# Halved first weight blocks in the projections, two norms made one stage earlier, semaphores cleared by range

## The reference

```python
h = rms_norm(x, mix_norm_g)
u = h @ w_in                                   # 1024 x 4096
dq, dk, dv, bq, bk, bv, z = split(u)
dq, dk, bq, bk = rms_norm of each over 64-wide heads
a = diff_attention(dq, dk, dv, lam, slopes)    # 4 heads; bias -slope * |distance|; softmax 1 - lam * softmax 2
b = dilated_attention(bq, bk, bv, slopes)      # 8 heads, windows 128/512/2048 at dilation 1/4/16
x = x + (concat(rms_norm(a) * 0.8, b) * silu(z)) @ w_out
x = x + sigmoid(rms_norm(x, ple_norm_g) @ w_ple_gate) * (p @ w_ple_proj)
# second block: sliding window attention with sinks
xn = rms_norm(x, norm_g_2)
q, k, v, z = split(xn @ a_w_in_2)
x = x + (banded_attention(q, k, v, t5_table, 128, sinks) * silu(z)) @ a_w_out_2
return rms_norm(x, final_g_2)
```

## Time and profile before

| what | value |
|---|---|
| median of 3 runs | 3131.64 us (3131.01 to 3131.96) |
| profiled execution | 3134.61 us, span 3132.8 us |
| TensorE products busy | 2984.1 us, 95% of the span |
| VectorE busy | 1656.2 us, 53% |
| ScalarE busy | 1195.8 us, 38% |
| GpSimd busy | 729.7 us, 23% |
| DMA | 302.94 MB, mean 97 GB/s |
| stages' ends (all engines meet) | p 786.0, d 1385.0, l 1754.0, m 1983.2, g 2235.7, s 2712.7, w 3128.9 |

### The profile page before, as it was taken

How to read it: one execution, slowest core, us unless ns; L and a number is a source line. 1 busy time by engine, 2 the same in 40 slices (tenths; PEclk the granted TensorE clock), 3 DMA queues, 4 the chain that set the end, 5 groups by cost and what they waited for, 6 DMA issues and landing times. The chain is left out here.

```text
span 3132.8 us, 47888 instructions
## 1 busy us (share of the span) xinstructions
PE 2984.1 (95%) x18330; PEld 2489.8 (79%) x18330; DVE 1656.2 (53%) x2757; ACT 1195.8 (38%) x2667; POOL 729.7 (23%) x576
## 2 busy tenths in 40 slices
PE   6999999999799999989999799899799999799998
PEld 6988888988588888878888678688688888667776
DVE  3366665000888888866666677433341100166665
ACT  3222221011577777755555321322211111255553
POOL 1234433110502010027452344200001110121111
PEclk9999999999899999999999899999899999899999
DMA  4212212223212010022332556332245542544341
GB/s 155 84 58 71 72 60 78 72 64 74 82 28 50 22 48 22 22 77 86 100 101 68 200 211 240 128 123 82 82 124 118 126 96 52 159 150 140 127 152 64
DMA packets 254270, 302.94 MB, mean 97 GB/s; under 512 B 19376, under 2 KB 201696, under 8 KB 250848
## 3 DMA queue, kind: packets, MB, share of 16 engines
q1 hardware_dynamic: 254048, 299.92, 31.7%
HBM read 190.38 MB, written 109.47 MB: 96 GB/s over the span
## 5 line engine op out<-in xcount | busy, mean ns | idle before, releaser
L890 DVE CUSTOM_DVE_ANT_0 d_e<-d_score,d_dist,d_slope 128x1024 f32<-128x1024 f32 x256 | 318.5, 1281 | 62.9 <-PE d_score L953 62.9
L561 PE MATMUL p_acc<-p_h_hi,p_w_hi 128*128 128x512 f32 x768 | 300.0, 391 | 1.0 <-issue 1.0
L561 PE MATMUL p_acc<-p_h_hi,p_w_lo 128*128 128x512 f32 x768 | 299.5, 390 | 0.0
L561 PE MATMUL p_acc<-p_h_lo,p_w_hi 128*128 128x512 f32 x768 | 299.1, 389 | 0.0
L812 ACT ACTIVATE d_e<-d_e,d_neg_top 128x2048 f32<-128x2048 f32 x128 | 257.0, 2008 | 86.5 <-DVE d_neg_top L899 86.2
L504 DVE RECIPROCAL p_root<-p_root 128x512 f32<-128x512 f32 x64 | 214.6, 3353 | 123.0 <-ACT p_root L417 123.0
L976 PE MATMUL d_out<-d_v,d_w_t 128*128 128x128 f32 x2048 | 251.5, 277 | 0.0
L976 PEld LDWEIGHTS d_out<-d_v,d_w_t 128*128 128x128 f32 x2048 | 240.9, 194 | 0.0
L561 PE MATMUL s_acc<-s_h_hi,s_w_hi 128*128 128x512 f32 x576 | 224.7, 390 | 0.0
L561 PE MATMUL s_acc<-s_h_hi,s_w_lo 128*128 128x512 f32 x576 | 224.4, 390 | 0.0
L561 PE MATMUL s_acc<-s_h_lo,s_w_hi 128*128 128x512 f32 x576 | 224.4, 390 | 0.0
(11 more groups left out here) (277 smaller groups left out, 6907.4 us busy)
## 6 DMA issues: line engine op xcount, KB each, us to landing
k_carry<-in_w_in SPq DMA_DIRECT2D x16, 1024.0 KB, 6.0
cols<-k_carry SPq DMA_DIRECT2D x64, 256.0 KB, 2.4
w_q<-q SPq DMA_DIRECT2D x15, 1024.0 KB, 7.8
k_carry<-x SPq DMA_DIRECT2D x27, 512.0 KB, 3.6
o_parts<-l_stage SPq DMA_DIRECT2D x192, 66.0 KB, 1.7
m_o<-o_parts SPq DMA_DIRECT2D x48, 264.0 KB, 6.0
k_carry<-cols SPq DMA_DIRECT2D x48, 256.0 KB, 4.6
k_carry<-in_a_w_in SPq DMA_DIRECT2D x10, 1024.0 KB, 5.6
```

The costliest lines, as they stand in the source:

```text
L561: mm = pe.matmul(acc[:, room], w_part[:, j, kt, ct * P:(ct + 1) * P], h_part[:, kt, tc * BANK:(tc + 1) * BANK], start=(kt == 0 and m == 0) ...
L890: dve.tensor_tensor_reduce(e[:, m % 3, s, half * HALF:(half + 1) * HALF], score[:, 2 * half:2 * half + 2].rearrange("p a b -> p (a b)"), d ...
```

## The change

Eight edits: (1) `Phase.clear` clears each run of neighbouring semaphore numbers with one instruction. (2) The first two weight blocks of a projection are loaded, rounded and subtracted in halves of four rows of 128; VectorE makes all four low halves, GpSimd none. (3) TensorE begins unit 0 with tile 0 and the first half of block 0; the transposes of tile 1 stand between the fourth and fifth step. A unit of the "rows" kind waits for each of its two tiles by itself. (4) `norm(t + 2)` no longer stands between the low parts of two tiles but behind both. (5) The eight gain loads move behind unit 7. (6) In the second projection the factors of tiles 2 to 15 are a power on GpSimd instead of root and reciprocal, and tiles 0 and 1 are normed in the gate stage, behind its tile 14. (7) The first k of diff attention is split in halves. (8) The fold of the distances goes to ScalarE as an absolute value; the signs of slope and of the diff gains are turned for it.

```diff
     def clear(self):
-        for counter in self.counters:
-            self.nc.gpsimd.sem_clear(counter)
+        nums = sorted(counter.num for counter in self.counters)
+        first = nums[0]
+        for num, following in zip(nums, nums[1:] + [None]):
+            if following != num + 1:
+                self.nc.gpsimd.sem_clear(range(first, num + 1))
+                first = following
...
     def load_w(self, sp, i):
-        sp.dma_start(self.w_raw[:, i % 2], self.w_b[self.blocks[i][0]]).then_inc(self.w_loaded[i % 2], 16)
+        src = self.w_b[self.blocks[i][0]]
+        if i < 2:
+            for half in range(2):
+                at = slice(4 * half, 4 * half + 4)
+                sp.dma_start(self.w_raw[:, i, at], src[:, at]).then_inc(self.w_first_loaded[2 * i + half], 16)
+        else:
+            sp.dma_start(self.w_raw[:, i % 2], src).then_inc(self.w_loaded[i % 2], 16)
...
# GpSimd, projection
-                invert_mean(0)
-                invert_mean(1)
-            make_lo(1)
+                for t in range(4):
+                    invert_mean(t)
+            else:
+                rest = inv[:, 2:NT]
+                pool.tensor_scalar(rest, sq_sums[:, 2:NT], 1.0 / D, EPS, ALU.mult, ALU.add).then_inc(rooted, 1)
+                pool.wait_ge(rooted, 1)
+                pool.tensor_tensor(rest, rest, half_down[:, 0:1].to_broadcast([P, NT - 2]), ALU.pow).then_inc(inverted, 1)
...
# ScalarE, projection
             if sq_sums is None:
                 square(0)
+            make_first_hi(0, 0)
+            make_first_hi(0, 1)
+            keep_hi(0)
+            if sq_sums is None:
                 square(1)
-            else:
-                act.activation(inv[:, 0], sq_sums[:, :], ACT.Sqrt, bias=eps[:, 0:1], scale=1.0 / D).then_inc(rooted, 1)
-            make_hi(0)
-            keep_hi(0)
-            make_hi(1)
+            make_first_hi(1, 0)
+            keep_hi(1)
+            make_first_hi(1, 1)
+            if sq_sums is None:
+                square(2)
+                square(3)
...
# VectorE, projection
-            norm(0)
-            norm(1)
-            dve.wait_ge(w_hi_made, 1)
-            dve.tensor_tensor(w_lo[:, 0], w_raw[:, 0], w_hi[:, 0].bitcast(F32), ALU.subtract).then_inc(w_lo_made, 1)
+            if sq_sums is None:
+                norm(0)
+            make_first_lo(0, 0)
+            keep_lo(0)
+            make_first_lo(0, 1)
+            if sq_sums is None:
+                norm(1)
+                make_first_lo(1, 0)
+                keep_lo(1)
+                make_first_lo(1, 1)
+                norm(2)
+                norm(3)
+            else:
+                norm(2)
+                keep_lo(1)
+                norm(3)
+                make_first_lo(1, 0)
+                make_first_lo(1, 1)
...
# TensorE, projection
                 for t in tiles_before(n):
-                    transposes(t)
-                pe.wait_ge(lo_kept, needs[n] + 1)
-                if n == first_of[i]:
-                    pe.wait_ge(w_lo_made, i + 1)
+                    if t != 1:
+                        transposes(t)
...
                     for two in range(2):
+                        pe.wait_ge(lo_kept, 2 * k + two + 1)
                         for kt in range(KT):
+                            if two == 0:
+                                wait_weights(n, i, kt)
+                            if n == 0 and two == 0 and kt == 4:
+                                transposes(1)
...
# diff attention, ScalarE (VectorE's fold and its whole-k subtraction go)
+            def fold(n, first, last):
+                act.wait_ge(counted, n + 1)
+                counts = e[:, 2].rearrange("p b n -> p (b n)")[:, first:last]
+                act.activation(dist[:, first:last], counts, ACT.Abs).then_inc(dist_made, 1)
+
             act.wait_ge(k_loaded, 64)
-            act.activation(k_hi[:, 0], k_raw[:, :], ACT.Copy).then_inc(k_hi_made, 1)
+            for s in range(2):
+                act.activation(k_hi[:, 0, s], k_raw[:, s], ACT.Copy).then_inc(k_first_hi, 1)
+            fold(0, NEAR, SPAN)
+            fold(1, 0, NEAR)
...
# gate stage, GpSimd
+            pool.wait_ge(squared, 2)
+            pool.tensor_scalar(first, sq_sums3[:, 0:2], 1.0 / D, EPS, ALU.mult, ALU.add).then_inc(next_set, 1)
+            pool.wait_ge(next_set, 2)
+            pool.tensor_tensor(first, first, swa_inputs.half_down[:, 0:1].to_broadcast([P, 2]), ALU.pow)\
+                .then_inc(next_rooted, 1)
...
# gate stage, VectorE
+                if isinstance(t, int) and t == NT - 2:
+                    dve.wait_ge(next_rooted, 1)
+                    dve.wait_ge(swa_inputs.gain_loaded, 16)
+                    for n in range(2):
+                        dve.wait_ge(swa_inputs.x_loaded[n], 16)
+                        dve.scalar_tensor_tensor(
+                            out=swa_inputs.x_slots[n], in0=swa_inputs.x_slots[n], scalar=swa_inputs.inv[:, n:n + 1],
+                            in1=swa_inputs.gain_all[:, :].rearrange("p (a b n) -> p a b n", a=2, n=P),
+                            op0=ALU.mult, op1=ALU.mult).then_inc(swa_inputs.first_normed, 1)
```

More of the change, by code:

```diff
@@ L317, in _ @@
                 inputs.load_x(sp, 2)
[L318 to L322, removed]
             for n, (i, k) in enumerate(units):
@@ L328, in _ @@
                 if n == first_of[i] and i + 2 < len(blocks):
-                    sp.wait_ge(w_lo_made, i + 1)
+                    sp.wait_ge(w_lo_made, 2 * (i + 1))
                     inputs.load_w(sp, i + 2)
+                if qk is not None and n == 8:
+                    for item, g in enumerate(qk):
+                        for half in range(2):
+                            sp.dma_start(g_raw[half * HD:(half + 1) * HD, item:item + 1], column(g),
+                                         allow_slow_non_contiguous=True).then_inc(qk_loaded, 16)
                 sp.wait_ge(staged[n % ROOMS], n // ROOMS + 1)
@@ L380, in _ @@
                     for t in tiles_before(n):
-                        if t + 2 < NT:
+                        if 2 <= t and t + 2 < NT:
                             invert_mean(t + 2)
@@ L470, in keep_lo, with make_first_lo @@
                                   h_hi[:, :, at].bitcast(F32), ALU.subtract).then_inc(lo_kept, 1)
-                if t + 2 < NT:
-                    norm(t + 2)
+            def make_first_lo(i, half):
+                at = slice(4 * half, 4 * half + 4)
+                dve.wait_ge(w_hi_made, 2 * i + half + 1)
+                dve.tensor_tensor(w_lo[:, i, at], w_raw[:, i, at], w_hi[:, i, at].bitcast(F32), ALU.subtract)\
+                   .then_inc(w_lo_made, 1)
             def fill_gains():
@@ L496, in _ @@
                 for t in tiles_before(n):
-                    keep_lo(t)
+                    if t >= 2:
+                        keep_lo(t)
+                for t in tiles_before(n):
+                    if 2 <= t and t + 2 < NT:
+                        norm(t + 2)
                 if kind == "head_norm":
@@ L524, in transposes @@
             def transposes(t):
-                pe.wait_ge(normed, t + 1)
+                if sq_sums is None:
+                    pe.wait_ge(normed, t + 1)
+                elif t < 2:
+                    pe.wait_ge(first_normed, t + 1)
+                else:
+                    pe.wait_ge(normed, t - 1)
                 if t >= 2:
@@ L851, in _ @@
         def _(dve):
-            def fold(n, first, last):
-                dve.wait_ge(counted, n + 1)
-                counts = e[:, 2].rearrange("p b n -> p (b n)")[:, first:last]
-                dve.scalar_tensor_tensor(out=dist[:, first:last], in0=counts, scalar=-1.0, in1=counts, op0=ALU.mult,
-                                         op1=ALU.min).then_inc(dist_made, 1)
             def lambda_sums():
@@ L871, in _ @@
             for h in range(DIFF_HEADS):
[L872 removed]
+                dve.memset(slope[:, h:h + 1], -(2.0 ** (-2 * (h + 1)))).then_inc(slope_set, 1)
             dve.wait_ge(q_first_hi, 1)
             dve.tensor_tensor(q_lo[:, 0], q_raw[:, 0], q_hi[:, 0].bitcast(F32), ALU.subtract).then_inc(q_first_made, 1)
[L875 to L877 removed]
+            for s in range(2):
+                dve.wait_ge(k_first_hi, s + 1)
+                dve.tensor_tensor(k_lo[:, 0, s], k_raw[:, s], k_hi[:, 0, s].bitcast(F32), ALU.subtract)\
+                   .then_inc(k_first_made, 1)
             dve.wait_ge(dist_made, 1)
@@ L931, in _ @@
                     lambda_sums()
-                    fold(1, 0, NEAR)
                     bias.fold_distance(dve)
@@ L943, in scores @@
                     wait_q_made(pe, n)
-                if m % NT == 0 and s == 0 and half == 0:
-                    pe.wait_ge(k_made, h + 1)
+                if m % NT == 0 and half == 0:
+                    wait_k_made(pe, h, s)
                 if 2 * m + s >= 1:
@@ L1954, in body @@
                 dve.tensor_tensor(new[:, par], new[:, par], xt[:, slot], ALU.add).then_inc(added, 1)
```

(4 more changed lines are left out.)

71 lines of the change are left out of this document (44 added, 27 removed).

## The result

The changed kernel takes 3116.6 us (median of six runs, 3112.6 to 3121.1), the kernel before on the same chips 3134.3 (3131.0 to 3139.1): ratio 0.9946, 95% interval 0.9933 to 0.9959, so 13 to 21 us faster. The difference of the medians is 17.7 us. Forecast were 3108.1 us and 23.5 us of gain, so the centre is 8.5 us off. The forecast's own range, 3104 to 3112, misses the median by 4.6 us. Only the range widened for rivals (a) and (b), 3102 to 3117, holds it, and that is luck: neither of the two came true. The profiled execution took 3117.88 us with a span of 3116.0, so it stands 16.8 us against the profiled one of before.

The account below looks back on a forecast made before the run. TensorE was taken as the bound inside every stage, so only its standstills at stage starts and the final clears counted: 10.0 + 2.6 + 0.8 + 6.5 + 3.6 = 23.5 us off 3131.64 gives 3108.1, range 3104 to 3112.

Parts of the forecast that it names:

- (a): Rival on the clears: a range costs per semaphore, so the gain is 17.7 us and the time 3113.9; chance 0.11.
- (b): Rival on both projections' heads: they gain half, 7.5 and 3.5 us, giving 18.0 in all and 3113.6; chance 0.15.
- First projection: Start of the first projection: TensorE starts at 15.15, unit 1 at 29.1 instead of 39.12; 10.0 us gained, bounds 7.5 and 11.5.
- Diff attention: Start of diff attention: split k and the fold on ScalarE bring the first bias earlier; 2.6 us gained, bounds 1.2 and 4.5.
- (c): Rival in diff attention: more VectorE mixes hit GpSimd's splits, up to 4.1 us each, so slower, up to 3169; chance 0.03.
- the row of 6.47: Profile row in diff attention: the longest mix takes 6.47 where the median is 2.34, so a hit costs up to 4.1.
- Dilated attention: Dilated attention: without the clears ahead of GpSimd's padding, VectorE goes on at once; 0.8 us gained, at least 0.
- clears: End of the kernel: a range clear costs as much as one, so 55 become two or three; 3.6 us gained.
- Second projection: Start of the second projection: unit 1 starts at 2254.0 instead of 2259.20; 6.5 us gained, bounds 3.5 and 8.5.

Follow-up runs that it names:

- e3: The changed kernel with two added GpSimd waits in diff attention: k_lo only after the mix of unit 4, 20 or 36, q_lo after the next; 3097.12 us, ratio 0.9887.
- e4: The kernel before with the same two GpSimd waits as e3; 3122.08 us, ratio 0.9966.
- e1: The kernel before with only the diff attention edits (k in halves, folds on ScalarE, signs); 3139.14 us against 3132.35, ratio 1.0016.
- e5: The kernel before with seven already satisfied TensorE waits (three instructions) at the start of diff attention; 3139.13 us against 3131.91, ratio 1.0023.
- e7: The kernel before with the range clears alone; 3129.9 us, ratio 1.0001.
- e2: The changed kernel with its diff attention as before; 3116.42 us, ratio 0.9948.
- e10: The changed kernel with the wait ahead of k_lo alone, that is e3 without the wait ahead of q_lo; 3101.3 us, ratio 0.9898.
- e6: The changed kernel with 504 TensorE waits for a value of 0 ahead of its first unit in the first projection; 3131.78 us.

## Why the prediction was right or wrong

**First projection, 10.0 forecast, 9.4 measured.** The halves landed as worked out (10.38 and 11.95 for 10.2 and 11.9), the first product came at 15.23 for 15.15, the second half of unit 0 at 22.06 for 22.7. Unit 1 came at 28.04, 1.1 earlier than I had it, since the transposes of tile 1 took 1.49, not 2.0, and its high and low parts followed sooner. The gain of 11.1 at that point then shrinks: between GpSimd's splits of two weight blocks lie 47.57 us, before 47.36, and in the seven steps from 176 to 509 this takes 1.5 of it back. It is the same in the seven profiles with the edits of the projection and in none of the others; the cause of these 0.2 us wasn't tried. So the forecast's "TensorE is busy to the end of the stage in both kernels" held, but its products came a little more slowly, and 9.4 for 10.0 is a head that gained 1.1 more and a rest that lost 1.7. Merge and gate (0.8 over) differ by as much from profile to profile.

**Diff attention, 2.6 forecast, lost 3.2 measured: the failed step.** Its sum was right in the main (a head 2.4 to 2.8 us shorter by the starts of the mixes, 2.7 by e3 against e4). One row in it was misread: the 1.42 from TensorE's start to "its first scores" is the start of the fourth pair of products, and the bias needs the end of the third, so the first bias gained 2.0, not 2.4. What failed is the dismissal of rival (c): "each split is released by TensorE's progress, so both move together". They do, but the release runs through SyncE's issue and a transfer, and these vary by 0.6 us and more where the order of the two operations was a matter of 0.3. I had the exclusion in my hands and had priced a hit at 4.1; with the low clock that follows, it is 5.5 to 7.0. I had treated the row of 6.47 as a rarity of 64, and not asked which units it struck: two of three heads, the third missed by 0.29 us. From that a case with its own chance follows: one more hit, 3108.1 + 5.5 = 3114. It is what came: of the 6.7 us by which the profiled execution missed its sum (16.8 for 23.5), this stage is 5.8.
That the folds bring no table load was taken for the 2.6 and stood in no row; the profile after shows none ahead of the folds, and one of 1.28 us ahead of the first exponential (783.21), as before (788.94). The exclusion itself held for the mix and k_lo in 24 cases of 24: in 20 the mix took 6.32 to 6.72 us for 2.34, in four k_lo took 6.50 to 6.58 for 4.55.

**The edit's worth depends on the tie.** Alone, the same edits made the kernel 6.8 us slower in the median (e1; 1 to 9 by the interval), three idle instructions 7.2 (e5). With the tie taken away the whole change gains 3122.08 - 3097.12 = 25.0 us, near the sum of 23.5.

**Dilated attention** (0.9 for 0.8) and the **clears** (3.5 for 3.6): in the profiles as forecast, and rival (a) fell: the four ranges at the end go by in 0.5 us. Two things are weaker than that sounds. The time of the kernel with the clears alone doesn't show their gain (e7), and the 0.9 came in seven profiles of eight with range clears (stage 368.2 to 368.6); in e7 a later rise of the clock took it. A range isn't quite as cheap as a single clear (median 89 ns against 44).

**Second projection, 6.5 forecast, 7.1 measured.** The power took 2.58 us for 2.3, but it held nothing up: VectorE's split ran inside it, 2230.62 to 2231.85, in 1.23 us. I had forecast that this split would wait for the power's end, carried over from the norm beside a subtraction; the measurement decides against it, in all seven profiles that have this power (the split took 1.22 to 1.23 us in each). In each of them the split started 0.5 us or more after the power did, so what an earlier start would meet isn't shown. The first product so came 4.4 us after the start of the stage, not 5.2. Unit 1 began at 2246.91, 17.5 after it (18.3 forecast, 23.5 before), and ended 23.4 after it. The 7.1 is one profile: over the seven with these edits the stage took 469.5 to 472.7, and in the two longest (e2 and e10) the clock rose 10.5 us or more after the stage's start, in the others 7.4 to 8.5. Rival (b) fell with both projections.

## What to carry to other kernels

Where one engine's long operation shuts another's out, ask of each meeting who starts first and by how much: under half a microsecond apart (0.39 before to 0.35 after in the table) it is a toss, and any edit ahead of it, even of instructions that do nothing, may turn it. Then a wait that fixes the order on the engine that has time (two waits, 17 us or more) is worth more here than shaving the head of the stage (2.7 us). When an edit that must gain comes out slower, count the long instances of one line before you doubt its sum.

## What the runs showed that was not expected

- A packet of q8, one of the two instruction queues, 0.3 to 0.5 us ahead of four DMA issues on SyncE goes with 2.88 to 3.13 us for the four, against 2.46 where it falls 1.4 to 1.7 us ahead (four kernels against eight at head 2). Three more instructions on TensorE moved it by 1.2 us, though they took 0.3 us themselves and TensorE stood waiting then; why it jumps was not tried, and that the packet itself slows the issue is not shown: the two go together in all twelve profiles.
- 504 waits for a value of 0, compiled to 252 instructions, took TensorE 27.3 us (3.0 to 30.3): 108 ns from one to the next. The stage grew by 20.0, since TensorE had stood idle for part of it.
- GpSimd's power of 14 columns (2.58 us) did not shut out a VectorE operation with two operands in SBUF, its subtraction of 2048 columns (4.55 us) did so each time that it started first.
- Runs of the kernel before spread over 18 us (29 runs, 3123.4 to 3141.4, with a granted clock of 0.974 to 0.981 over the whole run). With both waits it is 5.5 us in 5 runs (e3) and 7.5 in 9 (e4), so part of the spread may be the toss; but e6, where the toss stays, spread over 8.3 us in 12 runs, so this isn't shown.
- Another part lies elsewhere. The last stage has the same code in all twelve kernels and took 412.0 to 417.9 us in their profiles. In the shortest (e7) the granted clock of its first 50 us was 0.71, in the longest (e6) 0.57, and the others lie between these two. Differences of a few us between single profiles come from there as well.
